# A quad instead of direct units at the start of the second feed-forward block, with the output projection reordered

## The chip, the cores and the metric

The kernel runs on one core of a Trainium2 chip. The metric is the time of one execution on the device, in microseconds (us). Before the change the median of three runs is 987.46 us (987.20 to 988.02).

## The reference

One layer for 512 tokens of width 1024, in float32: a feed-forward block (FFN 1), a token-mixing stage, and a second feed-forward block (FFN 2), each added to x, and a final norm.

```python
def swiglu(h, w_gate, w_up, w_down):
    return (jax.nn.silu(h @ w_gate) * (h @ w_up)) @ w_down

x = x + 0.5 * swiglu(rms_norm(x, ffn1_norm[i]), ffn1_w_gate[i], ffn1_w_up[i], ffn1_w_down[i])
...                                   # SSD scan and pooled means of rms_norm(x) @ w_in
x = x + jnp.concatenate([y_ssd, y_pool], axis=-1) @ w_out[i]
x = x + 0.5 * swiglu(rms_norm(x, ffn2_norm[i]), ffn2_w_gate[i], ffn2_w_up[i], ffn2_w_down[i])
return rms_norm(x, final_norm)
```

The inner width D_FF is 2816, 22 tiles of 128.

## The kernel before

x is kept transposed: 8 tiles `xT` of 128 channels by 512 tokens. Every float32 matmul is made of three: the weights and the moving tensor are each split in a high part (ScalarE, a copy that rounds) and a low part (VectorE, the rest), and high times high, high times low and low times high are added. Converting weights is the function `convert` on both engines (`w_hi`, `w_lo`), in a ring of RING = 4 slots. Raw weights land in 8 slots of 512 KB through SyncE's queue. Engines meet by semaphores; the order on each engine is written out by hand.

The gate and up products of FFN 1 and 2 are made in two ways. A **direct** unit is one tile of gate or up: 8 blocks of weights, 24 matmuls of 512 columns. A **quad** makes gate and up of two tiles by seven products in place of eight (a Strassen-like scheme over two halves of the tokens and two halves of the channels). Its seven parts are A11, SUM1, SUM2, A12, SUM3, SUM4, A22, each 24 matmuls of 256 columns. A11, A12 and SUM4 read halves of the normed x; the others read token combinations `thi`, `tlo`, that are made once per block: for each j of four, ScalarE scales half a tile (`halves_of_x`), VectorE makes four terms (`combine`, line 1080), ScalarE their high part (`combination_hi`, line 748) and VectorE their low part (`combine_low`, line 1092), counted by `t_lo`. SUM1 to SUM4 use sums of weights that VectorE makes: `first_sum` (line 1102), `second_sum` (1112), `third_sum` (1118), `fourth_sum` (1124). Between the parts ScalarE copies banks out (`copy_product`, line 756) and VectorE adds others to them (`gather`, line 1131); GpSimd scales gates by the norm (`scale_gate`, line 611) behind each gather. TensorE may begin A22 only when the gather of SUM3 is done (`c22_done`), since both use one bank.

The norm is applied behind the products. Its statistics are made beside the work: ScalarE squares x (`square`, line 723), GpSimd adds the squares (line 599), TensorE sums over channels with a matmul against ones (`stat`, line 1631), ScalarE takes the root (`rms`, line 727) and VectorE the reciprocal (`inverse`, line 1052), which gates and directs need.

`DIRECT_TILES = (4, 2)`: FFN 1 makes its first four tiles by direct units, FFN 2 its first two (four units). In front of FFN 2 stand the eight units of the output projection over the SSD part (U_OUTS, weights `w_out[:, 0:DK]`), one for each tile d of x in the order 0 to 7. Behind each, VectorE adds the bank to x (line 1547), ScalarE makes the high part of the normed x (`norm_hi`) and the square, VectorE the low part (`norm_lo`), and both convert the weights of the unit four further on. The token combinations need tiles j and j + 4, so the four of them lie behind units 4 to 7; the last is made behind the last conversion.

The order in FFN 2 is that of `ffn(f, last)` on each engine: at item r ScalarE converts the weights of item r + 3, VectorE those of item r + 2, and a quad's sums come three, two and one items ahead of it.

## Time and profile before

| | us |
|---|---|
| median of 3 runs | 987.46 |
| the profiled execution | 987.8 |
| its span | 986.1 |
| TensorE busy | 976.8 |
| VectorE busy | 774.3 |
| ScalarE busy | 461.6 |
| GpSimd busy | 204.0 |

The span runs from the first to the last instruction of the profiled execution; 1.7 us of its time lie around it. Busy shares say which engine is full on the average. What a change in one place is worth is read from the timelines of that place: which wait ends last there. TensorE's granted clock was 0.998 of full speed.

### The profile page before, as it was taken

The numbers are of one execution on the slowest core, as the hardware profiler recorded it, in microseconds if no ns is written. First come the engines' busy times: TensorE is split into PE (matmuls) and PEld (weight loads), VectorE is DVE, ScalarE is ACT, GpSimd is POOL, SyncE is SP. The second block draws the span as 40 slices with busy tenths as digits, with TensorE's granted clock in tenths as the row PEclk, the third lists the DMA queues.
The fourth block names the chain that finished last, engine by engine and source line by source line (L and its number), as shares of the span: only waits on it lengthen the run. The fifth ranks groups of instructions, "written<-read, shape, count | busy, mean of one in ns | idle before, by whom it ended". The sixth has DMA issues, their size and how long they took to land.

```text
span 986.1 us, 15297 instructions
## 1 busy us (share of the span) xinstructions
PE 976.8 (99%) x6074; PEld 863.3 (88%) x6074; DVE 774.3 (79%) x985; ACT 461.6 (47%) x606; POOL 204.0 (21%) x172
## 2 busy tenths in 40 slices
PE   9999999999999999999999999999999999999997
PEld 7799889998999878878788778889988999889986
DVE  5888478985698788777799886798965899568964
ACT  6655225552355456552224653545532565325543
POOL 1003002220032222221064361201210223002321
PEclk9999999999999999999999999999999999999999
DMA  9526314563143343434443132263462335513412
GB/s 266 148 59 164 105 31 114 140 154 86 41 111 87 86 130 86 131 96 123 140 137 92 55 104 86 70 165 86 122 157 64 86 92 156 137 43 86 112 40 86
DMA packets 192271, 105.43 MB, mean 107 GB/s; under 512 B 4052, under 2 KB 189496, under 8 KB 192200
## 3 DMA queue, kind: packets, MB, share of 16 engines
q1 hardware_dynamic: 191528, 103.40, 37.6%
q8 instruction: 49, 0.80, 0.3%
q10 hardware_dynamic: 672, 1.05, 0.3%
q14 instruction: 22, 0.18, 0.1%
HBM read 102.30 MB, written 2.13 MB: 106 GB/s over the span
## 4 chain that ended last, share of the span: by engine, by line
PE 94%; DVE 5%; issue 1%; ACT 0%; DVEq 0%; POOL 0%; POOLq 0%
PE bank L1688 12%; PE bank L1690 12%; PE bank L1689 12%; PE bank L1623 9%; PE bank L1625 9%; PE bank L1624 9%; PE bank L1708 8%; PE bank L1707 8%; PE bank L1706 8%; PE bank L1778 1%; DVE w_lo_part L1041 1%; DVE ebuf L1375 1%; PE bank L1772 1%; PE bank L1775 1%; PE bank L1849 1%
## 5 line engine op out<-in xcount | busy, mean ns | idle before, releaser
L611 POOL TENSOR_TENSOR post<-post,rstd 128x256 f32<-128x256 f32 x57 | 93.1, 1633 | 516.2 <-DVE post L1131 516.2
L1688 PE MATMUL bank<-thi,w_hi_part 128*128 128x256 f32 x608 | 167.8, 276 | 0.0
L1689 PE MATMUL bank<-tlo,w_hi_part 128*128 128x256 f32 x608 | 167.8, 276 | 0.0
L1690 PE MATMUL bank<-thi,w_lo_part 128*128 128x256 f32 x608 | 167.8, 276 | 0.0
L1041 DVE TENSOR_TENSOR w_lo_part<-w_raw,w_hi_part 128x1024 fp32r<-128x1024 f32 (+1 forms) x102 | 128.9, 1264 | 16.9 <-ACT w_hi_part L699 14.7
L1706 PE MATMUL bank<-acthi,w_hi_part 128*128 128x512 f32 x340 | 132.7, 390 | 0.0
L1708 PE MATMUL bank<-acthi,w_lo_part 128*128 128x512 f32 x340 | 132.3, 389 | 0.0
L1707 PE MATMUL bank<-actlo,w_hi_part 128*128 128x512 f32 x340 | 132.3, 389 | 0.0
L1688 PE MATMUL bank<-xfhi,w_hi_part 128*128 128x256 f32 x418 | 115.6, 277 | 0.0
L1689 PE MATMUL bank<-xflo,w_hi_part 128*128 128x256 f32 x418 | 115.5, 276 | 0.0
L1690 PE MATMUL bank<-xfhi,w_lo_part 128*128 128x256 f32 x418 | 115.4, 276 | 0.0
L1689 PEld LDWEIGHTS bank<-tlo,w_hi_part 128*128 128x128 f32 x608 | 114.1, 188 | 0.0
L1688 PEld LDWEIGHTS bank<-thi,w_hi_part 128*128 128x128 f32 x608 | 114.1, 188 | 0.0
L1690 PEld LDWEIGHTS bank<-thi,w_lo_part 128*128 128x128 f32 x608 | 114.1, 188 | 0.0
L708 ACT ACTIVATE w_hi_part<-w_raw 128x1024 fp32r<-128x1024 f32 x76 | 80.3, 1057 | 71.8 <-PE bank L1690 36.8
L1036 DVE TENSOR_TENSOR w_lo_part<-w_raw,w_hi_part 128x1024 fp32r<-128x1024 f32 x76 | 106.1, 1402 | 0.0
L712 ACT ACTIVATE w_hi_part<-w_raw 128x1024 fp32r<-128x1024 f32 (+1 forms) x56 | 55.9, 998 | 105.2 <-PE bank L1708 70.0
L1172 DVE SCALAR_TENSOR_TENSOR upd<-bank,rstd 128x512 f32<-128x512 f32 x46 | 31.7, 690 | 89.5 <-PE bank L1708 89.5
L1623 PE MATMUL bank<-xmhi,w_hi_part 128*128 128x512 f32 x252 | 98.7, 392 | 0.0
L1625 PE MATMUL bank<-xmhi,w_lo_part 128*128 128x512 f32 x252 | 98.2, 390 | 0.0
L1624 PE MATMUL bank<-xmlo,w_hi_part 128*128 128x512 f32 x252 | 98.1, 389 | 0.0
L708 ACT ACTIVATE w_hi_part<-wsum 128x1024 fp32r<-128x1024 f32 x57 | 60.3, 1058 | 74.4 <-PE bank L1690 39.4
(293 smaller groups left out, 2082.7 us busy)
## 6 DMA issues: line engine op xcount, KB each, us to landing
w_raw<-in_ffn_w_gate SPq DMA_DIRECT2D x42, 512.0 KB, 4.0
w_raw<-in_ffn_w_up SPq DMA_DIRECT2D x42, 512.0 KB, 5.2
w_raw<-in_ffn_w_down SPq DMA_DIRECT2D x32, 512.0 KB, 5.1
w_raw<-in_w_in SPq DMA_DIRECT2D x29, 512.0 KB, 3.9
w_raw<-in_w_out SPq DMA_DIRECT2D x16, 512.0 KB, 4.0
w_raw<-in_ffn_w_down SPq DMA_DIRECT2D x16, 384.0 KB, 4.4
decay<-acs_rows SPq DMA_DIRECT2D x16, 256.0 KB, 4.6
out<-xtok SPq DMA_DIRECT2D x4, 512.0 KB, 2.6
```

Source lines behind the costliest of these rows:

```text
L708: act.activation(split(whi, n), weight(q, it.part), ACT.Copy).then_inc(w_hi, 1)
L1036: dve.tensor_tensor(split(wlo, n), weight(it.quad, it.part), split(whi, n).bitcast(F32), ALU.subtract).then_inc(w_lo, 1)
L1041: dve.tensor_tensor(wlo[:, slot(n), 0:blocks], raw[:, src, 0:blocks], whi[:, slot(n), 0:blocks].bitcast(F32), ALU.subtract).then_inc(w_lo, 1)
L1623: pe.matmul(bank, w, h, start=first and n == 0, stop=False)
L1624: pe.matmul(bank, w, l, start=False, stop=False)
L1625: mm = pe.matmul(bank, wl, h, start=False, stop=last and n == blocks - 1)
L1688: pe.matmul(out, w, hi, start=opens and e == 0 and k == 0, stop=False, skip_group_check=True)
L1689: pe.matmul(out, w, lo, start=False, stop=False, skip_group_check=True)
L1690: mm = pe.matmul(out, wl, hi, start=False, stop=end, skip_group_check=True)
L1706: pe.matmul(bank, whi[:, s, k, :], h, start=first and k == ks[0], stop=False)
L1707: pe.matmul(bank, whi[:, s, k, :], l, start=False, stop=False)
L1708: mm = pe.matmul(bank, wlo[:, s, k, :], h, start=False, stop=last and k == ks[-1])
```

## The change

`DIRECT_TILES` becomes (4, 0): FFN 2 has no direct units, and tiles 0 and 1 are a quad like the others, made behind the output projection at once. The output projection's units come in the order 0, 4, 1, 5, 2, 6, 3, 7, so that each odd unit completes a pair (j, j + 4); three combinations are made behind units 1, 3 and 5, the fourth behind the last one, where ScalarE makes its high part in front of the square and of the weights, and VectorE its low part in front of the weights. The first quad's first sum stands behind the fifth unit, its second sum behind the seventh, its third behind the last. The statistics matmul stands behind SUM1, the root at the third item of FFN 2 and the reciprocal at the fourth. TensorE makes the first quad's SUM1 block by block over both halves, and starts A11 when seven of the eight normed tiles are there.

```diff
-DIRECT_TILES = (4, 2)
+DIRECT_TILES = (4, 0)
...
+OUT_ORDER = (0, 4, 1, 5, 2, 6, 3, 7)
...
-            for i in range(DK):
-                mix_fetch(U_OUTS + i, w_out[:, 0:DK, block(i)])
+            for i, d in enumerate(OUT_ORDER):
+                mix_fetch(U_OUTS + i, w_out[:, 0:DK, block(d)])
...
# ScalarE
-                act.wait_ge(x_ready, DK * 2 * f + j + 1)
+                act.wait_ge(x_ready, DK * 2 * f + (1 + f) * j + 1)
...
-                    if f and it.kind == "direct" and it.raw == 0:
-                        combination_hi(1, KH - 1)
+                    if f and r == 2:
+                        rms(2)
...
-            for d in range(DK):
-                norm_hi(2, d, R_N2)
-                if d >= KH:
-                    halves_of_x(1, d - KH, R_N2)
-                square(2, d, d % 2, xT[:, cols(d)])
-                convert(M + U_OUTS + d + RING)
-                if d > KH:
-                    combination_hi(1, d - KH - 1)
-            rms(2)
+            for i, d in enumerate(OUT_ORDER):
+                if i % 2 == 0:
+                    halves_of_x(1, d, R_N2)
+                norm_hi(2, d, R_N2, seen=i)
+                if i == DK - 1:
+                    combination_hi(1, KH - 1)
+                square(2, i, i % 2, xT[:, cols(d)])
+                convert(M + U_OUTS + i + RING)
+                if i % 2 and i < DK - 1:
+                    combination_hi(1, i // 2)
...
# VectorE
-                    if f and it.kind == "direct" and it.raw:
-                        combine_low(1, it.raw)
+                    if f and r == 3:
+                        inverse(2)
...
-            for d in range(DK):
-                dve.wait_ge(unit_done, d + (M + U_OUTS + 1))
-                dve.tensor_tensor(xT[:, cols(d)], PB[4 + d % 2][:, :], xT[:, cols(d)], ALU.add).then_inc(x_ready, 1)
-                if d == KH + 1:
+            first = DIRECT_QUADS
+            for i, d in enumerate(OUT_ORDER):
+                dve.wait_ge(unit_done, i + (M + U_OUTS + 1))
+                dve.tensor_tensor(xT[:, cols(d)], PB[4 + i % 2][:, :], xT[:, cols(d)], ALU.add).then_inc(x_ready, 1)
+                if i == 1:
                     dve.wait_ge(neg_ready, 2)
-                if d > KH:
-                    combine(1, d - KH - 1, R_N2)
-                norm_lo(2, d, R_N2)
-                convert(M + U_OUTS + d + RING)
-            combine(1, KH - 1, R_N2)
-            combine_low(1, 0)
-            inverse(2)
+                if i == 6:
+                    second_sum(first)
+                if i % 2:
+                    dve.wait_ge(x_ready, i + (2 * DK + 1))
+                    combine(1, i // 2, R_N2)
+                elif i:
+                    combine_low(1, i // 2 - 1)
+                norm_lo(2, d, R_N2, seen=i)
+                if i == DK - 1:
+                    combine_low(1, KH - 1)
+                convert(M + U_OUTS + i + RING)
+                if i == 4:
+                    first_sum(first)
+            third_sum(first)
...
# TensorE
+                if n == M_FFN2:
+                    pe.wait_ge(xg_lo, 3 * DK - 1)
+                if f and local == 0 and part == A12:
+                    pe.wait_ge(xg_lo, 3 * DK)
+                order = [(e, k) for e in range(2) for k in range(KH)]
+                if f and local == 0 and part == SUM1:
+                    order = [(e, k) for k in range(KH) for e in range(2)]
...
-                        if n == M_FFN2:
-                            stat(2)
...
                         product(f, it, n)
+                        if n == M_FFN2 + SUM1:
+                            stat(2)
```

## Rows read from the trace of the kernel before

**Rows 1.** The page: busy time of each engine, and the chain that ended last, by engine.

```profile
PE 976.8 (99%) x6074; PEld 863.3 (88%) x6074; DVE 774.3 (79%) x985; ACT 461.6 (47%) x606; POOL 204.0 (21%) x172
...
PE 94%; DVE 5%; issue 1%; ACT 0%; DVEq 0%; POOL 0%; POOLq 0%
```

**Rows 2.** TensorE's timeline, 638 to 682 us: start us, duration us, engine, line, operation, count.

```profile
638.78 0.39 PE L1623 MATMUL bank<-x0hi,w_hi_part 128*128 128x512 f32 x1
...
644.36 1.02 PE L1631 MATMUL bank<-sumsq,ones 128*128 128x512 f32 x2
...
645.45 0.40 PE L1624 MATMUL bank<-x0lo,w_hi_part 128*128 128x512 f32 x1
...
662.00 0.28 PE L1688 MATMUL bank<-x0hi,w_hi_part 128*128 128x256 f32 x1
...
681.08 0.28 PE L1688 MATMUL bank<-x0hi,w_hi_part 128*128 128x256 f32 x1
```

**Rows 3.** Busy time of each engine in two stretches (columns in the first line).

```profile
core 0: us, PE busy (x) PEld busy (x) DVE busy (x) ACT busy (x) POOL busy (x), PEclk, DMA share, GB/s
600.90:638.98 38.08, 38.08 (x169) 31.54 (x168) 24.93 (x29) 18.45 (x26) 9.86 (x7) 1.00 0.23 66
...
681.04:700.10 19.06, 19.06 (x170) 19.06 (x170) 18.21 (x20) 11.09 (x14) 4.64 (x3) 1.00 0.37 104
```

**Rows 4.** VectorE's timeline after the last output-projection unit, 639 to 648 us.

```profile
638.98 0.69 DVE L1547 TENSOR_TENSOR xT<-bank,xT 128x512 f32<-128x512 f32 x1
639.59 0.87 DVE L1080 SCALAR_TENSOR_TENSOR t<-xT,par,b 128x256 f32<-128x256 f32 x2
...
641.30 0.74 DVE L1046 SCALAR_TENSOR_TENSOR xflo<-xT,par,xfhi 128x512 fp32r<-128x512 f32 x1
642.34 1.94 DVE L1041 TENSOR_TENSOR w_lo_part<-w_raw,w_hi_part 128x1024 fp32r<-128x1024 f32 x1 [0.29 <-ACT w_hi_part L712]
...
647.04 3.35 DVE L1052 RECIPROCAL rstd<-sq 128x512 f32<-128x512 f32 x1
```

**Rows 5.** ScalarE's timeline, 640 to 669 us.

```profile
640.74 0.61 ACT L723 ACTIVATE sq<-xT 128x512 f32<-128x512 f32 x1
641.26 1.04 ACT L712 ACTIVATE w_hi_part<-w_raw 128x1024 fp32r<-128x1024 f32 x1
642.21 1.04 ACT L748 ACTIVATE thi<-t 128x1024 fp32r<-128x1024 f32 x1
645.42 0.69 ACT L727 ACTIVATE sq<-bank,eps 128x512 f32<-128x512 f32 x1 [2.17 <-PE bank L1631]
...
667.68 0.60 ACT L756 ACTIVATE post<-bank 128x512 f32<-128x512 f32 x1 [1.17 <-PE bank L1690]
668.18 1.05 ACT L708 ACTIVATE w_hi_part<-wsum 128x1024 fp32r<-128x1024 f32 x1
```

**Rows 6.** VectorE's timeline, quad of tiles 2 and 3 and the next, 673 to 693 us.

```profile
673.12 0.69 DVE L1131 TENSOR_TENSOR post<-post,bank 128x512 f32<-128x512 f32 x1 [2.63 <-PE bank L1690]
673.73 1.22 DVE L1102 TENSOR_TENSOR wsum<-w_raw 128x1024 f32<-128x1024 f32 x1
674.86 1.76 DVE L1036 TENSOR_TENSOR w_lo_part<-w_raw,w_hi_part 128x1024 fp32r<-128x1024 f32 x1
...
677.15 1.21 DVE L1112 TENSOR_TENSOR wsum<-w_raw,wsum 128x1024 f32<-128x1024 f32 x1
...
679.96 0.67 DVE L1131 TENSOR_TENSOR post<-post,bank 128x512 f32<-128x512 f32 x1
...
692.20 0.69 DVE L1131 TENSOR_TENSOR post<-post,bank 128x512 f32<-128x512 f32 x1 [0.84 <-PE bank L1690]
```

**Rows 7.** GpSimd's timeline: a sum of squares, and a gate scaling.

```profile
641.51 1.68 POOL L599 TENSOR_TENSOR sumsq<-sumsq,sq 128x512 f32<-128x512 f32 x1 [3.75 <-ACT sq L723]
673.95 1.59 POOL L611 TENSOR_TENSOR post<-post,rstd 128x256 f32<-128x256 f32 x1 [30.76 <-DVE post L1131]
```

**Rows 8.** The SyncE queue's timeline: issue of the weights of FFN 2.

```profile
622.18 0.58 SPq L468 DMA_DIRECT2D w_raw<-in_ffn_w_up  x1
```

**Rows 9.** The page's DMA issues: KB each, median us from issue to landing.

```profile
w_raw<-in_ffn_w_up SPq DMA_DIRECT2D x42, 512.0 KB, 5.2
```

More of the change, by code:

```diff
@@ L712, in convert, with norm_hi @@
                     act.activation(whi[:, slot(n), 0:blocks], raw[:, it.raw % RAW, 0:blocks], ACT.Copy).then_inc(w_hi, 1)
-            def norm_hi(p, d, gain):
-                act.wait_ge(x_ready, d + (DK * p + 1))
+            def norm_hi(p, d, gain, seen=None):
+                act.wait_ge(x_ready, (d if seen is None else seen) + (DK * p + 1))
                 act.activation(normed(p)[0][d], xT[:, cols(d)], ACT.Copy,
@@ L1042, in convert, with norm_lo @@
                                       whi[:, slot(n), 0:blocks].bitcast(F32), ALU.subtract).then_inc(w_lo, 1)
-            def norm_lo(p, d, gain):
-                dve.wait_ge(xg_hi, d + (DK * p + 1))
+            def norm_lo(p, d, gain, seen=None):
+                dve.wait_ge(xg_hi, (d if seen is None else seen) + (DK * p + 1))
                 dve.scalar_tensor_tensor(out=normed(p)[1][d], in0=xT[:, cols(d)], scalar=par[:, one(d + gain)],
@@ L1637, in direct @@
                     pe.wait_ge((g_scaled, act_ready)[it.part], tile - 1)
-                products(PB[bank][:, :], n, 0, UB, *normed(2 * f), ready=(xg_lo, 2 * DK) if n == M_FFN2 else None)
+                products(PB[bank][:, :], n, 0, UB, *normed(2 * f))
             def moving(f, part, k):
@@ L1679, in product @@
                 pe.wait_ge(w_lo, n + 1)
-                for e in range(2):
-                    out = bank[:, half(e)]
-                    for k in range(KH):
-                        if part == SUM1 and local == 0 and e == 0:
-                            pe.wait_ge(t_lo, KH * f + k + 1)
-                        hi, lo = moving(f, part, k)
-                        w, wl = whi[:, slot(n), e * KH + k, :], wlo[:, slot(n), e * KH + k, :]
-                        end = k == KH - 1
-                        pe.matmul(out, w, hi, start=opens and e == 0 and k == 0, stop=False, skip_group_check=True)
-                        pe.matmul(out, w, lo, start=False, stop=False, skip_group_check=True)
-                        mm = pe.matmul(out, wl, hi, start=False, stop=end, skip_group_check=True)
+                if n == M_FFN2:
[5 more added lines that the diff above has]
+                    order = [(e, k) for k in range(KH) for e in range(2)]
+                for i, (e, k) in enumerate(order):
+                    out = bank[:, half(e)]
+                    if part == SUM1 and local == 0 and e == 0:
+                        pe.wait_ge(t_lo, KH * f + k + 1)
+                    hi, lo = moving(f, part, k)
+                    w, wl = whi[:, slot(n), e * KH + k, :], wlo[:, slot(n), e * KH + k, :]
+                    end = k == KH - 1
+                    pe.matmul(out, w, hi, start=opens and i == 0, stop=False, skip_group_check=True)
+                    pe.matmul(out, w, lo, start=False, stop=False, skip_group_check=True)
+                    mm = pe.matmul(out, wl, hi, start=False, stop=end, skip_group_check=True)
                 mm.then_inc(unit_done, 1)
```

## The prediction, made before the change was run

> **What bounds the kernel now.** First the page: TensorE is busy 976.8 of 986.1 us, and the chain that ended last is 94% TensorE's own work, 5% VectorE's [rows 1]. Matmul work that is taken away is therefore worth its full time, unless an engine that feeds TensorE becomes late in the same place. Then TensorE's timeline where FFN 2 begins: the first direct unit starts at 638.78, the first quad at 662.00, the second quad at 681.08, and TensorE never waits [rows 2]. The next view is VectorE's busy time in stretches. In the output projection it works 24.93 of 38.08 us; in the second quad of FFN 2, 18.21 of 19.06 [rows 3]. So VectorE has room in front of FFN 2 and about 0.8 us per quad within it. Last come the timelines of VectorE and ScalarE around the step [rows 4 to 6]: what has to happen between the last token sum and the point where a quad's last part may start.
>
> **What is removed and added on TensorE.** Tiles 0 and 1 took four direct units of 24 matmuls of 512 columns, with the statistics matmul between two of them: 662.00 − 638.78 = 23.22 us [rows 2]. One unit is 644.36 − 638.78 = 5.58 us, so four are 22.32, and the statistics with the restart behind them are the other 0.90. A quad is 7 parts of 24 matmuls of 256 columns: 681.08 − 662.00 = 19.08 us [rows 2], 2.73 per part. The statistics remain. With no wait the stretch becomes 19.08 + 0.90 = 19.98 us, **3.24 us less**. This is the whole possible gain.
>
> One rule speaks against it. The Trainium skill ("TensorE: Matmul & The Clock Gate", section "The mechanism") says that a weight load overlaps running matmuls only where its row group differs, and here all weights fill 128 rows. By that, halving the columns would not halve the spacing; the row does not agree, as 168 matmuls each with weights of its own start 0.114 us apart [rows 2], about half of the direct unit's 0.233. I take the row.
>
> **The output projection.** Units keep their count and size; they are made in the order 0, 4, 1, 5, 2, 6, 3, 7, and the weight fetches follow, so SyncE's queue issues as many transfers at the same places. Three of the four token combinations (1.71 us each on VectorE, from 639.59 to 641.30 [rows 4]), three of their low parts (1.14 each, the spacing that 673.73 to 674.86 shows for 1,024 elements [rows 6]) and two weight sums of 1.14 run inside the eight units. Even without counting that three combinations ran there before, 3 × 1.71 + 3 × 1.14 + 2 × 1.14 = 10.8 us fit VectorE's 13.15 idle us [rows 3]. The first sum is VectorE's at the fifth unit and waits for weights whose last transfer is issued at 622.18 and takes about 5.2 us [rows 8, 9], so they are there at 627.4; VectorE reaches the sum at about 627.5 by its order (add from 622.7, low part, norm, conversion, with 0.4 lost to GpSimd). Behind that wait stand the sixth and seventh adds, for which TensorE has a unit of 5.4 us in hand. The seventh has 4.6 us of work and ends at about 638.7, just before the eighth add at 638.98. Cost on the path: nothing. If the landing is later by L, what follows is later by L minus some 0.3.
>
> **Behind the last unit: the new path.** Before, the reciprocal of the norm (3.35 us, [rows 4]) was needed only for posting direct units. Now it stands in VectorE's queue inside the first quad, at the fourth part, and the first gather, the next quad's first sum, the conversion for the quad's last part and the second gather are queued behind it. TensorE may not start the last part (A22) before the second gather. Step by step:
>
> - VectorE adds at 638.98 and combines to 641.40 (0.61 + 0.1 for its own semaphore + 1.71) [rows 4].
> - ScalarE's high part takes 1.04 [rows 5]: 642.5. VectorE's low part: 643.8. TensorE is at the fourth block of SUM1 at 638.78 + 2.73 + 18 × 0.114 = 643.55: **wait 0.3**.
> - ScalarE squares (0.52) and converts (1.04) [rows 5], done at 644.0. GpSimd's sum of squares overlaps; before, the conversion beside it took 1.94 [rows 4, 7] where 1.22 is normal, so 0.7 to 0.8 more at most. I take 645.7 for the conversion's end and 644.8 for GpSimd's, where SUM1 ends at 644.55: **wait 0.2** for the statistics.
> - Third sum to 646.85; ScalarE converts it to 647.95, copies a bank (0.50, the spacing 667.68 to 668.18), converts SUM4's weights to 649.5 and takes the root (0.69) to 650.2 [rows 5]. VectorE meanwhile makes the fourth sum and one conversion, then SUM4's conversion from 649.55 to 650.7.
> - Reciprocal to 654.05, the first gather from **654.1**. TensorE had finished that bank (A12) at 638.78 + 4 × 2.73 + 0.3 + 0.2 + 0.9 = 651.1.
> - From the first gather to the end of the second VectorE needs 677.15 − 673.12 = 4.03, one gate scaling of GpSimd included [rows 6, 7]. A22 can start at 654.1 + 4.03 + 0.1 = 658.2. TensorE is ready at 651.1 + 2 × 2.73 = 656.6: **wait 1.6**.
> - The next quad's first weights are there 679.96 − 673.12 = 6.84 behind the gather [rows 6]: 661.0. A22 ends at 660.95: **wait 0.1**.
>
> Waits together 2.2 to 2.3, so the second quad starts at 661.05 where it was 662.00 [rows 2]: **0.95 us sooner**. Then VectorE's work from gather to gather is 692.20 − 0.84 − 673.12 = 18.24 [rows 6], so the next first gather comes at 672.4 while A12 of that quad ends at 661.05 + 10.9 = 671.95: 0.4 late. From a quad's A12 to its A22 TensorE has two parts, 5.46, and the two gathers need 4.13 of them, so a lag up to 1.3 costs nothing. The backlog is gone one quad later, and the rest of the kernel is only shifted.
>
> **GpSimd's port.** The rows show a conversion of 1.76 instead of 1.22 behind a gate scaling [rows 6], 0.54 lost, though GpSimd shows 1.59 us [rows 7]. The Trainium skill ("SBUF — State Buffer", section "SBUF: two separate sides") calls the port pair that VectorE and GpSimd share an exclusive lock, held for a whole instruction, the other one blocked. Taken at GpSimd's full 1.6 us, each of the three encounters on the path would cost 1.05 more, and the sum would turn from 0.95 less to about 2.2 more. The trace agrees with a block but not with its length: most of GpSimd's 1.59 is itself waiting. I take 0.54 for a scaling and up to 0.8 for a sum.
>
> **The forecast** against the profiled execution (987.8, of which the span is 986.1) is 986.85; against the median of 987.46, 0.34 lower, it is **986.5**.
>
> **Rivals.**
>
> 1. *No wait is made: 984.2.* If VectorE reached the first gather at 652.4 or sooner, A22 would not wait, and with SUM1's and the statistics' waits gone too the full 3.24 would remain. For it: the order puts most token sums in front. Against: the chain has a fixed 3.35 reciprocal and three hand-overs to ScalarE of 1.1 each after a sum that can't start before 638.98. A part of it (hand-overs quicker than I put them, no loss to GpSimd) gives 985 to 985.5. Chance 0.18 for all that is under 985.5.
> 2. *The backlog doesn't heal: 990.* VectorE enters the chained quads 1 to 3 us late and needs 18.24 of each 19.08 [rows 6]. If its work per quad grows by over 0.8 (more lost to GpSimd, whose scalings would now fall beside other instructions), the lag stays, and each of the next two quads waits another 1.7 before A22: −0.95 + 2 × 1.7 = +2.45, 989.9. For it: 0.8 is little room. Against: the same instructions in the same order ran in 18.21 us in a quad without a wait [rows 3]. Between this and the forecast lies a late landing of the weights at the fifth unit: 3 us later would bring +1.7. Chance 0.08 for over 989.4, and 0.08 for 987.7 to 989.4.
> 3. *The change does not do what it says.* The direct units go for certain; but if the eighth sum's order bought nothing, SUM1 would wait for it at its start rather than at its fourth block: 0.3 more becomes 2.3. That would only move the wait forward, as VectorE and ScalarE set A22, so at most 0.3 is added: 986.8, within the forecast.
>
> **Chances.** The forecast (985.5 to 987.7) 0.66, rival 1 0.18, the stretch up to 989.4 0.08, rival 2 0.08. About 0.2%, 2 us, is what a measurement of this kernel can tell from no change. Faster by more (under 985.5): 0.18. Slower by more (over 989.4): 0.08. Within: 0.66 + 0.08 = 0.74. The range takes in the bounds of the hand-overs (eight of 0.06 to 0.15), of GpSimd (nothing to 1.05 more at one encounter) and half of each neighbouring case: 984.6 to 988.4.
>
> **What would show it.** In the new trace: the second quad starts at about 661 (right) or 658.8 (rival 1); TensorE is idle about 1.6 us in front of A22, at VectorE's gather, and 0.2 to 0.3 in front of SUM1's fourth block; the reciprocal starts at 650.7; the first gather of the second quad starts within 0.5 us of its bank. Wrong would be: idle time of TensorE in the output projection, a first sum that waits for its weights past 628, a wait before A22 in the third quad, or a reciprocal that starts before 649.

## The result: 1.3 us slower, where 1.0 less was forecast

| | before | after |
|---|---|---|
| median of 20 runs, us | 987.45 | 988.76 |
| lowest and highest | 987.00, 988.03 | 988.06, 989.81 |
| after / before | | 1.0012 (1.0006 to 1.0017) |
| the profiled execution | 987.8 | 989.81 |
| its span | 986.1 | 988.1 |

The change costs 0.13%. That is inside the 0.2% that the prediction called no change, but the interval excludes 1, the time lies outside the predicted range of 984.6 to 988.4, and the sign is the opposite of the forecast. The profiled execution is the slowest of its 20; the part of it that belongs to that execution alone is separated below.

First the page of after (busy time of each engine; the chain that ended last, by engine):

```profile
PE 976.2 (99%) x6146; PEld 866.3 (88%) x6146; DVE 786.9 (80%) x995; ACT 466.2 (47%) x612; POOL 209.0 (21%) x175
...
PE 90%; DVE 7%; issue 1%; DMA 1%; ACT 0%; POOL 0%; DVEq 0%; SPq 0%; POOLq 0%
```

Against [rows 1], TensorE lost 4 points of the chain, VectorE gained 2, and a DMA is in it, where none was. TensorE's busy time is only 0.6 lower, though matmuls worth 3.24 us went, and its idle time grew from 9.3 to 11.9 (span less busy). The page can't say where, so the stretch must be read. TensorE's waits between 636 and 665 us, from the view of waits (engine, what waited, its line, whom for: us in total, times, longest):

```profile
PE bank L1706 <- DVE post L1135: 1.0, 1, 1.0
PE bank L1706 <- DVE tlo L1096: 0.8, 1, 0.8
PE bank L1706 <- DVE xflo L1050: 0.7, 1, 0.7
PE bank L1643 <- POOL sumsq L602: 0.2, 1, 0.2
```

And where they stand in its timeline (last matmul of the output projection, A11, SUM1's fourth block, the statistics, A22, then the second and the third quad):

```profile
638.77 0.39 PE L1637 MATMUL bank<-mixhi,w_lo_part 128*128 128x512 f32 x1
639.85 0.36 PE L1706 MATMUL bank<-x0hi,w_hi_part 128*128 128x256 f32 x1 [0.69 <-DVE xflo L1050]
...
645.68 0.38 PE L1706 MATMUL bank<-thi,w_hi_part 128*128 128x256 f32 x1 [0.78 <-DVE tlo L1096]
...
646.82 1.12 PE L1643 MATMUL bank<-sumsq,ones 128*128 128x512 f32 x2 [0.17 <-POOL sumsq L602]
...
660.28 0.38 PE L1706 MATMUL bank<-thi,w_hi_part 128*128 128x256 f32 x1 [1.03 <-DVE post L1135]
...
663.21 0.33 PE L1706 MATMUL bank<-x0hi,w_hi_part 128*128 128x256 f32 x1
...
683.05 0.28 PE L1706 MATMUL bank<-x0hi,w_hi_part 128*128 128x256 f32 x1
```

The output projection ends at 638.77 + 0.23 = 639.00, so the stretch to the second quad is 663.21 − 639.00 = 24.2 us, where before had 23.22 [rows 2] and I forecast 22.27. It can be split at two points, the start of VectorE's eighth add (of a bank of the projection to x) and the start of TensorE's A22:

| us | forecast | after | after again (e1) | e2 | e3 |
|---|---|---|---|---|---|
| end of the projection to the eighth add | 0.20 | 1.76 | 1.79 | 0.82 | 0.20 |
| eighth add to A22 | 19.2 | 19.52 | 19.53 | 19.53 | 18.78 |
| A22 to the second quad | 2.85 | 2.93 | 2.91 | 2.91 | 2.91 |
| the stretch | 22.27 | 24.2 | 24.2 | 23.3 | 21.9 |

Four fifths of the miss are in the first line, in work that I had priced at nothing. Here is VectorE's timeline of after in the output projection:

```profile
619.87 1.79 DVE L1050 SCALAR_TENSOR_TENSOR xflo<-xT,par,xfhi 128x512 fp32r<-128x512 f32 x1
621.59 1.21 DVE L1045 TENSOR_TENSOR w_lo_part<-w_raw,w_hi_part 128x1024 fp32r<-128x1024 f32 x1
...
624.76 0.75 DVE L1050 SCALAR_TENSOR_TENSOR xflo<-xT,par,xfhi 128x512 fp32r<-128x512 f32 x1
...
628.62 1.23 DVE L1106 TENSOR_TENSOR wsum<-w_raw 128x1024 f32<-128x1024 f32 x1 [0.84 <-DMA w_raw<-in_ffn_w_up]
629.77 0.69 DVE L1552 TENSOR_TENSOR xT<-bank,xT 128x512 f32<-128x512 f32 x1
...
632.20 1.79 DVE L1050 SCALAR_TENSOR_TENSOR xflo<-xT,par,xfhi 128x512 fp32r<-128x512 f32 x1
...
637.92 1.78 DVE L1050 SCALAR_TENSOR_TENSOR xflo<-xT,par,xfhi 128x512 fp32r<-128x512 f32 x1
...
640.76 0.68 DVE L1552 TENSOR_TENSOR xT<-bank,xT 128x512 f32<-128x512 f32 x1
```

The low part of the normed x takes 0.75 us, or 1.79: three times (fourth, sixth and seventh unit) it lies beside GpSimd's add of squares, and loses 1.04. (At the second unit a combination's last two terms lose as much, 2.13 for 1.00 at 608.13, and VectorE catches up.) GpSimd and SyncE's queue at the same places:

```profile
619.56 1.55 POOL L602 TENSOR_TENSOR sumsq<-sumsq,sq 128x512 f32<-128x512 f32 x1 [3.74 <-ACT sq L726]
...
631.89 1.55 POOL L602 TENSOR_TENSOR sumsq<-sumsq,sq 128x512 f32<-128x512 f32 x1 [5.19 <-ACT sq L726]
637.57 1.58 POOL L602 TENSOR_TENSOR sumsq<-sumsq,sq 128x512 f32<-128x512 f32 x1 [4.12 <-ACT sq L726]
```

```profile
622.83 0.37 SPq L471 DMA_DIRECT2D w_raw<-in_ffn_w_gate  x1
623.24 0.58 SPq L471 DMA_DIRECT2D w_raw<-in_ffn_w_up  x1
```

The first meeting, at 619.87, makes the conversion behind it end 1.04 later, at 622.8. The slot that it frees is the target of the transfer at 622.83. The one for which the first sum waits stands behind that in SyncE's queue, so it is issued at 623.24 instead of 622.18 [rows 8] (0.2 of this is the later end of the projection in this execution), and the sum waits 0.84 us for it. The second and third meeting take the room in which VectorE would have caught up: from sixth to seventh add it needs 635.05 − 629.77 = 5.28 us, from seventh to eighth 5.71, where TensorE's unit takes 5.44.

Why did before not show 1.04? VectorE's conversion beside GpSimd's add at the fourth and at the sixth unit, in the kernel before:

```profile
620.18 1.56 DVE L1041 TENSOR_TENSOR w_lo_part<-w_raw,w_hi_part 128x1024 fp32r<-128x1024 f32 x1 [0.72 <-ACT w_hi_part L699]
...
631.46 1.95 DVE L1041 TENSOR_TENSOR w_lo_part<-w_raw,w_hi_part 128x1024 fp32r<-128x1024 f32 x1 [0.30 <-ACT w_hi_part L712]
```

At the fourth unit VectorE waited 0.72 us for ScalarE while GpSimd's add was under way, and the conversion lost 0.34 (1.56 for 1.22). At the sixth and seventh, where a combination already stood in front, the wait was 0.30 and the conversion lost 0.73. In the reordered code the token combinations and the sums fill the waits, and the loss is 1.04 each time. VectorE's work in the projection was 24.93 us [rows 3]; now it is 32.15 (columns as there):

```profile
601.12:639.00 37.88, 37.88 (x168) 31.16 (x166) 32.15 (x37) 19.93 (x28) 9.72 (x7) 1.00 0.23 65
```

### The profile page after: what moved, and what is told of

The parts are those of the page before. It is cut to its first block, busy times and chain, and to the rows that moved or that the text cites. A ratio compares the mean times of both kernels' runs of the same rounds, so it can differ in the third digit from the quotient of the medians.

```text
span 988.1 us, 15481 instructions
## 1 busy us (share of the span) xinstructions
PE 976.2 (99%) x6146; PEld 866.3 (88%) x6146; DVE 786.9 (80%) x995; ACT 466.2 (47%) x612; POOL 209.0 (21%) x175
## 3 DMA queue, kind: packets, MB, share of 16 engines
q10 hardware_dynamic: 672, 1.05, 0.3%
HBM read 102.30 MB, written 2.13 MB: 106 GB/s over the span
## 4 chain that ended last, share of the span: by engine, by line
PE 90%; DVE 7%; issue 1%; DMA 1%; ACT 0%; POOL 0%; DVEq 0%; SPq 0%; POOLq 0%
PE bank L1706 13%; PE bank L1707 13%; PE bank L1708 13%; PE bank L1726 8%; PE bank L1724 8%; PE bank L1725 8%; PE bank L1635 7%; PE bank L1637 7%; PE bank L1636 7%; PE bank L1796 1%; DVE w_lo_part L1045 1%; DVE ebuf L1379 1%; PE bank L1790 1%; PE bank L1793 1%; DVE t L1084 1%
## 5 line engine op out<-in xcount | busy, mean ns | idle before, releaser
L1706 PE MATMUL bank<-thi,w_hi_part 128*128 128x256 f32 x640 | 177.5, 277 | 1.8 <-DVE post L1135 1.0
L1707 PE MATMUL bank<-tlo,w_hi_part 128*128 128x256 f32 x640 | 176.9, 276 | 0.0
L1708 PE MATMUL bank<-thi,w_lo_part 128*128 128x256 f32 x640 | 176.9, 276 | 0.0
L1045 DVE TENSOR_TENSOR w_lo_part<-w_raw,w_hi_part 128x1024 fp32r<-128x1024 f32 (+1 forms) x98 | 120.8, 1234 | 13.5 <-ACT w_hi_part L702 13.3
L1706 PEld LDWEIGHTS bank<-thi,w_hi_part 128*128 128x128 f32 x640 | 120.2, 188 | 2.4 <-DVE post L1135 1.2
L1706 PE MATMUL bank<-xfhi,w_hi_part 128*128 128x256 f32 x440 | 121.9, 277 | 0.0
L1707 PE MATMUL bank<-xflo,w_hi_part 128*128 128x256 f32 x440 | 121.8, 277 | 0.0
L1708 PE MATMUL bank<-xfhi,w_lo_part 128*128 128x256 f32 x440 | 121.7, 277 | 0.0
L1708 PEld LDWEIGHTS bank<-thi,w_lo_part 128*128 128x128 f32 x640 | 120.4, 188 | 0.0
L1040 DVE TENSOR_TENSOR w_lo_part<-w_raw,w_hi_part 128x1024 fp32r<-128x1024 f32 x80 | 113.2, 1421 | 1.0 <-ACT w_hi_part L711 1.0
```

Of the source, the lines that this page charges most:

```text
L1040: dve.tensor_tensor(split(wlo, n), weight(it.quad, it.part), split(whi, n).bitcast(F32), ALU.subtract).then_inc(w_lo, 1)
L1045: dve.tensor_tensor(wlo[:, slot(n), 0:blocks], raw[:, src, 0:blocks], whi[:, slot(n), 0:blocks].bitcast(F32), ALU.subtract).then_inc(w_lo, 1)
L1706: pe.matmul(out, w, hi, start=opens and i == 0, stop=False, skip_group_check=True)
L1707: pe.matmul(out, w, lo, start=False, stop=False, skip_group_check=True)
L1708: mm = pe.matmul(out, wl, hi, start=False, stop=end, skip_group_check=True)
```

## The experiments

The medians of before on the same chips were 987.86 to 987.91. A ratio is to them, with its interval. Waits and stretches come from each kernel's own trace, that of one execution. Times in two traces can be compared only against the end of the projection. It lies between 638.05 and 639.23 in the traces of before, after, e1 to e3, e5, e6 and e8 to e12, and nearly all of this difference is made in the first 8 us: TensorE's first matmul on the normed x starts between 7.08 and 8.24.

**e1: the changed kernel once more.** In after, the quad that starts at 663.21 takes 683.05 − 663.21 = 19.84 us with no wait, where a quad took 19.08 [rows 2]. Does that belong to the kernel?

> The changed kernel once more, for its profile and as the measure for the others. What is open: in the first profile the parts of 24 matmuls of 256 columns took 2.82 us from 647.4 to 684 (0.1178 us a matmul) where the kernel before has 2.72 (0.1133). Theory A, the slower spacing belongs to this order of work: it is there again, over both first quads, and the time is 1.2 to 1.5 us over the kernel before. Theory B, it is an accident of one execution (that one took 989.81, the median is 988.76): the spacing is 0.1133 after the last wait, and the span is about 1 us shorter than 988.1. In both the eighth token sum starts at about 640.7, a good 1.5 us later than it would without the first sum's wait for weights and the meetings with GpSimd.

Measured: 988.38 against 987.86, ratio 1.0008 (0.9999 to 1.0017). Second and third quad of e1, TensorE's timeline:

```profile
662.80 0.36 PE L1706 MATMUL bank<-x0hi,w_hi_part 128*128 128x256 f32 x1
...
681.95 0.28 PE L1706 MATMUL bank<-x0hi,w_hi_part 128*128 128x256 f32 x1
```

19.15 us: theory B. Thus 0.7 of the 2.0 us by which after's span is longer belongs to that one execution; 0.2 more lie in front of the stretch (639.00 against 638.78), and 1.0 is the stretch. The stretch in front is the same 24.2 in both, and so are the lateness of the eighth add (1.79) and the wait for the weights. The cost of the change that repeats is 1.0 us in this stretch; the medians give 1.3 and 0.5. From the third quad to the end all the traces named above agree within 0.1 us.

**e2: the transfer that the first sum needs is fetched first.** The four tiles of the first quad's weights are fetched in another order, so that the late slot takes a tile that is needed later.

```diff
-                        for j in range(4):
+                        for j in ((3, 0, 1, 2) if f and it.raw == 0 else range(4)):
                             fetch((f, it.raw + j), (wg, wu)[j % 2][f][:, :, block(it.tile + j // 2)])
```

> The changed kernel with the transfers of the first quad's weights issued in the order 3, 0, 1, 2 in place of 0, 1, 2, 3: the slot of transfer 3 is free first. Only one transfer, not two, is then issued behind the fourth unit's conversion. Theory L (the first sum's wait for weights makes VectorE late): the wait of 0.84 us at 628.6 goes, the sixth add starts at about 628.9 instead of 629.8, the eighth at 640.0 or sooner instead of 640.76, and 0.7 to 0.9 us of time go. Theory G (the meetings with GpSimd and the added work alone make it late): the wait goes, but the eighth add stays within 0.3 us of 640.7 and the time within 0.3.

Measured: 987.97 against 987.86, 1.0003 (0.9994 to 1.0012). VectorE's first sum, sixth, and eighth add:

```profile
626.76 1.21 DVE L1106 TENSOR_TENSOR wsum<-w_raw 128x1024 f32<-128x1024 f32 x1
627.89 0.68 DVE L1552 TENSOR_TENSOR xT<-bank,xT 128x512 f32<-128x512 f32 x1
...
638.87 0.68 DVE L1552 TENSOR_TENSOR xT<-bank,xT 128x512 f32<-128x512 f32 x1
```

The wait for the weights is gone, and so is TensorE's before A11. The eighth add is 0.82 behind its unit instead of 1.79, and the stretch is 23.3. Everything behind the add is unchanged, to A22 at add + 19.53. So the wait for the weights is worth 1.0 us of the stretch (0.4 in the medians, 987.97 against e1's 988.38); 0.6 of the lateness is left, which the transfer does not explain.

**e3: GpSimd's adds in the second norm take one column.** The sums of squares of the other columns are left out.

```diff
-                    pool.tensor_tensor(sumsq[:, :], sumsq[:, :], sq[:, e, :], ALU.add).then_inc(sum_own, 1)
+                    w = 1 if p == 2 else S
+                    pool.tensor_tensor(sumsq[:, 0:w], sumsq[:, 0:w], sq[:, e, 0:w], ALU.add).then_inc(sum_own, 1)
```

> The changed kernel in which GpSimd adds the squares of the second norm for one column of 512 alone, so that its eight adds behind the token sums no longer hold VectorE; this leaves out the norm of all other columns. Theory G: the low parts of x that took 1.79 us at the fourth, sixth and seventh sum take 0.75, the eighth add comes 1.5 us sooner, at about 639.2, TensorE does not wait at A11, and the time falls by 1.5 to 2 us. Theory L: the waits for weights stay as they are (0.84 us, or more, since VectorE comes there sooner), the eighth add moves by 0.7 us or less and the time falls by under 0.8.

Measured: 986.63 against 987.86, 0.9991 (0.9981 to 1.0000). VectorE:

```profile
619.26 0.75 DVE L1051 SCALAR_TENSOR_TENSOR xflo<-xT,par,xfhi 128x512 fp32r<-128x512 f32 x1
...
626.83 1.22 DVE L1107 TENSOR_TENSOR wsum<-w_raw 128x1024 f32<-128x1024 f32 x1
...
638.58 0.69 DVE L1553 TENSOR_TENSOR xT<-bank,xT 128x512 f32<-128x512 f32 x1 [0.68 <-PE bank L1638]
```

With the transfers in the order of after, the wait for the weights is gone too: the slot came free in time (issue at 621.59). VectorE now waits for TensorE at the seventh and eighth add: it is in time, as I had forecast. So without GpSimd's adds the whole lateness of 1.56 to 1.59 is gone, and the late transfer was their consequence. The stretch is 21.9, 0.4 less than my forecast; the meeting behind the eighth add (1.99 for a conversion of 1.23) is gone as well.

**e12: the same edit in the kernel before**, as a control: perhaps these adds cost there too.

> The control for e3_nosum: the kernel before with GpSimd's eight adds of squares of the second norm cut to one column (the norm of the others is left out). If GpSimd's hold on VectorE matters only where VectorE has become the one that is late, the time is that of the kernel before within 0.2 us, and all of the 1.75 us that e3 gained on the changed kernel were made by the change. If it falls by 0.5 us or more, the adds cost the kernel before as well.

Measured: 987.78 against 987.91, 1.0000 (0.9991 to 1.0009), stretch 661.28 − 638.06 = 23.2, no wait of TensorE. The adds cost the kernel before nothing that can be measured. The 1.75 us by which e3 beats the changed kernel (e1, 988.38 in the same set) is a cost that the change brought out. The trace shows also how far spans differ with an equal stretch: e12's is 985.4 and before's 986.1, and the 0.7 is there at the first matmul on the normed x (7.09 and 7.82) and at the end of the projection (638.06 and 638.78).

**e5: a short reciprocal.** It takes 64 of 512 columns; the others keep the scale of an earlier norm.

```diff
-                dve.reciprocal(rstd[:, :], sq[:, 0, :]).then_inc(rstd_ready, 1)
+                w = 64 if p == 2 else S
+                dve.reciprocal(rstd[:, 0:w], sq[:, 0, 0:w]).then_inc(rstd_ready, 1)
```

> The changed kernel with VectorE's reciprocal of the second norm cut from 512 to 64 columns (3.35 us to about 0.6; the other columns keep the scale of the norm before). Theory V (everything up to A22 hangs on VectorE's queue from the eighth add on, 19.53 us in two profiles): A22 starts at the eighth add plus 16.8, so TensorE waits 0.3 us or not at all there in place of 1.0 to 1.7, the second quad starts at about 661 in a profile in which it was 662.8, and the time falls by 1.4 to 2.0 us to about 986.6. Rival S (ScalarE's conversions or the bank copies hold A22 as well): A22 moves by under 0.8 us and the time falls by under 0.8.

Measured: 987.17 against 987.87, 0.9991 (0.9981 to 1.0000). VectorE's reciprocal and first gather:

```profile
652.72 0.55 DVE L1057 RECIPROCAL rstd<-sq 128x64 f32<-128x64 f32 x1
653.48 0.69 DVE L1136 TENSOR_TENSOR post<-post,bank 128x512 f32<-128x512 f32 x1 [0.21 <-DVE rstd L1057]
```

TensorE's waits:

```profile
PE bank L1707 <- DVE tlo L1097: 0.8, 1, 0.8
PE bank L1707 <- DVE xflo L1050: 0.7, 1, 0.7
PE bank L1644 <- POOL sumsq L602: 0.2, 1, 0.2
```

The gather comes 2.6 us sooner, the wait before A22 is gone, and the stretch is 661.38 − 638.96 = 22.4. That VectorE's queue (reciprocal, gather, gather) sets A22 holds. The stretch is 1.8 shorter than in e1, and not by the 2.8 that the reciprocal lost: only by what TensorE had waited there (the gap of 1.61 in e1 and the restart behind it). The medians fell by 1.2, less than the 1.4 to 2.0 expected.

**e6: the new order with the direct units kept.** `DIRECT_TILES` is (4, 2), and sums, statistics, root and reciprocal stand where they were.

```diff
-DIRECT_TILES = (4, 0)
+DIRECT_TILES = (4, 2)
...
-                if i == 6:
-                    second_sum(first)
...
-                if i == 4:
-                    first_sum(first)
-            third_sum(first)
+            inverse(2)
```

> The new order of the output projection's units and of the token combinations alone, with the four direct units of FFN 2 kept, the weight sums, the statistics, the root and the reciprocal where they were. Theory G: VectorE meets GpSimd's adds here too (1.79 us for a low part in place of 0.75 at the fourth, sixth and eighth unit), but nothing waits for weights, the eighth add starts within 0.5 us of its unit, TensorE waits under 0.3 us, and the time is that of the kernel before within 0.4 us (987.5 to 988.3 where before is 987.86). Rival O (the reordering itself costs): TensorE waits a microsecond or more in front of FFN 2 or in the first direct unit, and the time is 1 us or more above before.

Measured: 988.80 against 987.87, 1.0008 (0.9999 to 1.0017), where I expected at most 0.4 us; the stretch is 24.0 instead of 23.2. VectorE's eighth add, then TensorE's timeline, GpSimd's and ScalarE's:

```profile
639.43 0.69 DVE L1549 TENSOR_TENSOR xT<-bank,xT 128x512 f32<-128x512 f32 x1 [0.54 <-PE bank L1630]
```

```profile
644.58 0.40 PE L1630 MATMUL bank<-xfhi,w_lo_part 128*128 128x512 f32 x1
645.50 0.70 PE L1636 MATMUL bank<-sumsq,ones 128*128 128x512 f32 x1 [0.52 <-POOL sumsq L602]
```

```profile
643.73 1.72 POOL L602 TENSOR_TENSOR sumsq<-sumsq,sq 128x512 f32<-128x512 f32 x1 [5.92 <-ACT sq L726]
```

```profile
641.99 1.06 ACT L751 ACTIVATE thi<-t 128x1024 fp32r<-128x1024 f32 x1 [1.11 <-DVE t L1083]
642.95 0.62 ACT L726 ACTIVATE sq<-xT 128x512 f32<-128x512 f32 x1
```

The eighth add is on time here (0.2 behind its unit), though two low parts of x take 1.79 here too: with no weight sums in VectorE's queue, it catches up. So it takes both to make it late, GpSimd's adds and the moved sums; e3 took away the one, e6 the other. What costs here is that ScalarE makes the combination's high part before the square: GpSimd starts 643.73 − 639.43 = 4.3 us behind the eighth add, where it was 2.5 [rows 4, 7], and the statistics matmul waits. With the direct units kept, the reordering costs 0.8 to 0.9. In the changed kernel the statistics stand behind SUM1, and the same order costs a wait of 0.2 there.

**e9: the square before the high part**, in the changed kernel:

```diff
+                square(2, i, i % 2, xT[:, cols(d)])
                 if i == DK - 1:
                     combination_hi(1, KH - 1)
-                square(2, i, i % 2, xT[:, cols(d)])
```

> The changed kernel with one exchange: behind the eighth token sum ScalarE makes the square before the combination's high part, not after it. ScalarE is idle there for 1.1 us, so the square should cost it nothing, and GpSimd's last add comes 1.6 us sooner. Theory G: TensorE's wait for the statistics (0.2 us) goes, VectorE loses its microsecond to GpSimd at the last low part of x instead of at the conversion, SUM1's fourth block is 0.3 to 0.6 us later, and the time stays within 0.4 us of the changed kernel (988.4). Rival: the exchange frees TensorE of what the new order cost with the direct units kept (0.8 us at the statistics), and the time falls by 0.5 us or more.

Measured: 988.49 against 987.91, 1.0006 (0.9997 to 1.0015). The wait for the statistics is gone, SUM1's grows from 0.8 to 1.3, and A22's is 0.4 (1.0 in after, 1.4 in e1). The stretch is 23.65, 0.6 less than in e1, but the median is not lower: the exchange moves the wait and gains at most that 0.6. It was not run with the direct units kept.

**e7 and e10: no long reciprocal at all, with e2's fetch.** The root and reciprocal are taken of 128 x 4 values, one for each token, and spread again by a float32 matmul against diagonal blocks.

```diff
+                            for b in range(NC):
+                                mm = pe.matmul(PB[6][:, b:b + 1], sumsq[:, block(b)], ones[:, 0:1], start=True, stop=True)
...
+                        dve.reciprocal(tok_rms[:, 1, :], tok_rms[:, 0, :]).then_inc(inv_made, 1)
...
+                        if n == M_FFN2 + SUM3:
+                            pe.wait_ge(diag_made, NC)
+                            pe.matmul(PB[6][:, :], ones[:, :], sq[:, 0, :], start=True, stop=True).then_inc(spread_done, 1)
```

> The changed kernel with the transfers in the order 3, 0, 1, 2, and the second norm's scale made by tokens: four matmuls of one column bring the sums to 128 tokens by 4, ScalarE takes the root of 4 columns, VectorE the reciprocal of 4 columns (0.2 us in place of 3.35), ScalarE scales four blocks of the identity, TensorE spreads them with one float32 matmul of 512 columns behind SUM3, and ScalarE copies the bank. TensorE has the same float32 work, ScalarE some 1.8 us more, VectorE 3.2 less. Theory V: no wait in front of A22, the second quad starts about 1.2 us sooner than in the kernel before against the same end of the output projection (22.0 instead of 23.2 us), and the time is about 986.7. Rival S: ScalarE's additional work makes the bank copies late, TensorE waits 1 us or more at SUM3, SUM4 or the next quad's SUM2, and the time is 987.9 or above.

Measured: 987.48 against 987.87, 1.0000 (0.9990 to 1.0009). Its trace is that of an execution of 5.6 ms and is not read here, so the kernel ran once more:

> The kernel e7_rt once more, for a profile (the one before was taken in an execution of 5.6 ms). Expected as before: no wait in front of A22, waits in front of SUM1's fourth block and the statistics (0.8 and 0.2), the second quad 22.0 us behind the end of the output projection; a time 0.3 to 0.5 us under the kernel before, as measured once.

Measured: 987.46 against 987.91, 0.9998 (0.9989 to 1.0007). TensorE's waits:

```profile
PE bank L1720 <- DVE tlo L1107: 0.7, 1, 0.7
PE bank L1756 <- POOL sumsq L603: 0.2, 1, 0.2
```

A22 does not wait, and the stretch is 661.30 − 638.74 = 22.6: 0.7 less than in e2, and 0.5 less in the medians. It was expected at 22.0, and the time at 986.7 (e7). What remains is SUM1's wait for the last low part and the 0.2 at the statistics.

**e8: also the last combination in two steps**, so that SUM1 gets its first term early (diff of the high part; the low part is split in the same way):

```diff
+                if f and j == KH - 1:
+                    act.wait_ge(t_own, 4 * (KH * f + j) + 1)
+                    act.activation(thi[:, 0, j, :], t32[:, j, 0, :], ACT.Copy).then_inc(t_hi, 1)
+                    act.wait_ge(t_own, 4 * (KH * f + j + 1))
+                    act.activation(thi[:, 1:4, j, :], t32[:, j, 1:4, :], ACT.Copy).then_inc(t_hi, 1)
+                    return
```

> The one before, and the last pair's combination in two steps: its first term, which alone SUM1 reads, is split by ScalarE and VectorE in front of the other three. Theory V with the second wait of the changed kernel, the one in front of SUM1's fourth block (0.8 to 1.0 us), taken away: SUM1 runs without a wait or with under 0.2, and the time is 0.7 to 0.9 us below the one before, about 985.9. Rival T: the statistics, which wait for GpSimd's last add (about 2.3 us behind the high part of the eighth tile), stand directly behind SUM1, so the wait moves there and the gain is under 0.3 us.

Measured: 988.14 against 987.87, 1.0006 (0.9997 to 1.0015); stretch 22.8, where e10 has 22.6. SUM1 no longer waits, and the statistics behind it wait for all of it, as the expectation's rival T said:

```profile
PE bank L1773 <- POOL sumsq L603: 1.3, 1, 1.3
```

**e11: as e8, with the square between the two steps.**

> The kernel e8_full with the square of the eighth tile made between the two steps of the last combination, so that GpSimd's last add, for which TensorE waited 1.3 us there, comes about 1 us sooner. Theory V and G together: the only waits left are some 0.3 us at the statistics, the second quad starts 21.0 to 21.5 us behind the end of the output projection (23.2 in the kernel before, 24.2 in the changed one), and the time is 1.5 us or more under the kernel before, about 986.2. Rival P (pauses of whatever kind make TensorE's matmuls stand further apart for a while, by chance): the waits go as expected, but the parts behind the statistics still take 2.82 us in place of 2.72, and the time is 987 or more.

Measured: 987.18 against 987.91, 0.9996 (0.9987 to 1.0006): the lowest median of a complete kernel, but its interval holds 1. The expected 986.2 was not reached. Neither wait is left, and a third takes their place, of SUM2 for ScalarE's copy of a bank. Behind it the granted clock fell (TensorE's timeline):

```profile
643.66 0.95 PE L1775 MATMUL bank<-ones,sumsq 128*128 128x1 f32 x8
645.65 0.39 PE L1739 MATMUL bank<-thi,w_hi_part 128*128 128x256 f32 x1 [1.04 <-ACT post L767]
```

And three windows, with the columns of [rows 3]:

```profile
636.00:643.60 7.60, 7.60 (x59) 7.14 (x58) 7.35 (x10) 2.69 (x5) 2.70 (x2) 1.00 0.56 154
646.60:649.90 3.30, 3.30 (x18) 3.30 (x17) 3.04 (x4) 2.57 (x4) 0.00 (x0) 0.50 0.09 24
650.00:660.00 10.00, 10.00 (x83) 9.52 (x83) 8.11 (x9) 5.89 (x10) 2.63 (x2) 1.00 0.64 175
```

Before the fall TensorE had 2.0 us of one-column matmuls and waiting. From 646.60 to 649.90 the granted clock was 0.50, the lower of its two levels (1.2 of 2.4 GHz), and the matmuls stand 0.213 us apart instead of 0.113; 24 matmuls took 4.5 us instead of 2.7. The stretch is 23.9 in this execution, so its saving was spent.

The clock of whole executions fits this. Of e11's eleven, the three with a mean granted clock of 0.997 or 0.998 took 987.93 to 988.36 us, the eight with 0.999 took 986.99 to 987.46. In e8 the six with 0.997 or 0.998 took 988.14 to 989.64, the five with 0.999 at most 987.66. A mean of 0.997 occurs in e7, e8, e10 and e11, the kernels with the one-column matmuls, 12 times, and in no execution of any other kernel. No trace but e11's shows where in the kernel the clock was lost.

**e4: what makes the spacing wide?** The kernel before, with four pauses of TensorE and one float32 matmul put in by hand:

```diff
+                if f == 1 and tile0 == 4 and part == A12:
+                    pe.wait_ge(u2_read, q + 1)
+                if f == 0 and tile0 == 10:
+                    if part == SUM1:
+                        pe.wait_ge(p1_read, q + 1)
...
+                if f == 1 and tile0 == 10 and part == A12:
+                    pe.wait_ge(rstd_ready, 3)
+                    pe.matmul(PB[6][:, :], ones[:, :], rstd[:, :], start=True, stop=True)
```

> The kernel before with three probes on TensorE in quads that run without a wait there, all operations the same but one. In FFN 1, quad of tiles 10 and 11, SUM1, SUM2 and A12 each wait for ScalarE's copy of the part before (about 0.7 us of idle each); in FFN 2, quad of tiles 4 and 5, A12 waits so once; in FFN 2, quad of tiles 10 and 11, a float32 matmul of ones with 512 columns stands in front of A12 with no wait. Theory I (an idle TensorE runs its matmuls further apart for a while after): the spacing behind the waits is 0.1178 instead of 0.1133 us for 20 us or more. Theory F (the float32 matmul does it): 0.1178 behind the float32 matmul alone, 0.1133 behind the waits. Theory N (neither, but something of the first quads' place): 0.1133 behind all of them. The waits cost about 2.8 us together by themselves.

Measured: one run, 993.37. Behind the first pause of FFN 1 (162.32) the matmuls stand 0.1177 us apart, behind the second (166.11) 0.1141, behind the third (169.83) 0.1133. Behind the pause in FFN 2 (692.96) they stand 0.1175 to 0.1179 apart for 14 us, and behind the float32 matmul at 794.30, which waited for nothing, for 15 us. The granted clock does not show it:

```profile
693.20:704.30 11.10, 11.10 (x96) 11.10 (x96) 9.18 (x11) 4.32 (x5) 3.36 (x3) 1.00 0.68 187
707.10:717.00 9.90, 9.90 (x89) 9.90 (x89) 9.27 (x12) 7.17 (x10) 0.72 (x1) 1.00 0.12 33
```

So a pause and a float32 matmul can each bring the wide spacing, not every pause does (behind e1's longest, 1.4 us, the matmuls stand narrow), and another pause can end it. None of the three expected theories holds as it was put, and each probe was seen in one execution only.

## Why the prediction was wrong, point by point

- **"3.24 us less" of TensorE's work: right.** In e1 TensorE's four gaps (0.88, 0.95, 0.33, 1.61) and 0.1 more at each restart behind them give 4.2 us, and 24.2 less these is the 20.0 of the sum.
- **"The output projection … Cost on the path: nothing": wrong, and this is the step that failed.** The term for GpSimd's adds was mis-sized there. "0.4 lost to GpSimd" was put to the fifth unit alone, and there it came true (1.55 for a conversion of 1.21). The meetings at the fourth, sixth and seventh unit, where the moved combinations and sums take VectorE's waits away, had next to nothing: the seventh's "4.6 us of work" is the sum of its instructions without a loss. The measured loss is 1.04 for each of the three, 3.1 us together, and the eighth add comes 1.76 behind its unit where 0.20 was forecast. The sum of idle time (13.15 us for 10.8 of work) was too coarse as well: after has 37.88 − 32.15 = 5.7 us left, most of it before the fourth unit, and from the sixth add on none.
- **The prices on the path behind the eighth add held.** Each gate scaling cost a conversion 0.54 (1.76), and the last add of squares 0.77 (1.99 for 1.22), where "up to 0.8" was allowed; the 1.05 more of the rival rule is not seen there. It was in front of the eighth add that it was seen. The rows show 1.55 us of GpSimd beside 1.04 lost by VectorE. The Trainium skill ("SBUF — State Buffer", section "SBUF: two separate sides") speaks of an exclusive lock for the whole instruction. The trace agrees with a lock and nearly with its length where VectorE's instruction starts right behind GpSimd's: the low part starts 0.31 after GpSimd's add, and of the 1.24 us that are left of this add VectorE loses 1.04. I was wrong to apply the rule, and a price of my own, only behind the last unit.
- **"If the landing is later by L": the mechanism stood in the text, its cause did not.** The weights came at 628.6, past the 628 that I named as wrong. Against 627.4 that is an L of 1.2, which by the rule of 0.3 less would cost 0.9; e2 gained 1.0. I had counted the transfer's issue (622.18) as fixed; it follows a slot, and so a conversion of VectorE's. e2 and e3 show it from both sides.
- **The chain behind the eighth add: right.** Forecast 19.2 from add to A22, measured 19.52 and 19.53; reciprocal at add + 11.7, measured 11.98. The wait before A22 (1.6 forecast) is 1.0 in after and 1.4 in e1. The two differ by the wide spacing of after's matmuls in front of it (0.1178 us from 648 to 659), which let TensorE come later. The waits at SUM1's fourth block and at the statistics (0.3 and 0.2) measured 0.8 and 0.2; the order did put SUM1's wait at its fourth block, so rival 3 did not come.
- **"The backlog is gone one quad later": right**, and rival 2 did not come: TensorE waits for nothing in the second and third quad.
- **Rival 1** needed a gather at 652.4. e5 brought it to 653.5 and had no wait at A22, but 22.4 us and not 19.98: the waits in front are not removed by a quicker gather.
- **What no step had:** 0.7 us of wide spacing in the profiled execution, and the price of putting ScalarE's high part before the square (0.8 in e6). In the changed kernel the latter is small, as predicted: the statistics wait 0.2.

From the forecast of 22.27 to the 24.2 measured: 1.56 for the eighth add (gone without GpSimd's adds, by e3; 1.0 of it by way of the late transfer, by e2), 0.3 in the chain, 0.1 at the restart behind A22.

Open: why the medians differ by 1.3 in the first set and 0.5 in e1's. Two things that vary between executions are of that size, the wide spacing (0.7 in one quad) and the first 8 us of the kernel (1.2 us between the earliest and the latest trace); how often each comes is not known, as a trace shows one execution only. Most of the medians here have intervals that hold 1, so the causes rest on the traces. It was not tried to have the squares summed by another engine, or to leave the weight sums where they were with the quad kept.

## What to carry to other kernels

Idle time of VectorE can be GpSimd's time at the port. Before work is moved into it, look at what GpSimd does in these microseconds, and take the price of a meeting from a row where both engines work back to back, not from one where one of them was idle in front. A transfer's issue time is no constant either: follow the slot that it fills back to the instruction that frees it. And where short waits follow one another, removing one may be worth little: e2 and e5 shortened the stretch by what was waited there (1.0 and 1.8), but in e8 and e11 the next wait took the place of the one removed.

## What the runs showed of the hardware that was not expected

- **Two spacings at full clock.** The quads' matmuls of 256 columns, each with its own weights, stand 0.1133 us or 0.1177 us apart, both at a granted clock of 1.00. The wide one came behind some pauses of 0.7 to 1.0 us and behind some float32 matmuls, lasted 8 to 14 us where neither a pause nor a float32 matmul followed and about 37 us in after (with A22's pause in it), and costs 0.7 us per quad. The same kernel had it in one execution (19.84 us for a quad) and not in another (19.15). What decides it is open.
- **VectorE's loss to GpSimd** for one and the same add of 128 x 512: 1.04 us where VectorE's next instruction starts 0.3 us behind it with no wait in front, 0.73 with a wait of 0.30 and 0.34 with a wait of 0.72 in front.
- **The granted clock fell to 0.50** for 3.3 us, 0.9 us behind the end of 2.0 us of one-column matmuls and waiting (e11), and stayed at 1.00 behind single pauses of 1.0 us (e4).
